# Eight tokens' gated one-hots made by one wide comparison and one wide product, in a Trainium2 decoder layer

## What is computed

```python
def peer_ffn(h, w_q, sub_keys1, sub_keys2, u_tab, v_tab):
    ...
    v1, i1 = lax.top_k(s1, PEER_TOPK)          # 16 of 128 keys, first half
    v2, i2 = lax.top_k(s2, PEER_TOPK)          # 16 of 128 keys, second half
    cand = (v1[..., :, None] + v2[..., None, :]).reshape(B, S, PEER_HEADS, PEER_TOPK * PEER_TOPK)
    cand_id = (i1[..., :, None] * N_KEYS + i2[..., None, :]).reshape(B, S, PEER_HEADS, PEER_TOPK * PEER_TOPK)
    top_s, pos = lax.top_k(cand, PEER_TOPK)
    ids = jnp.take_along_axis(cand_id, pos, axis=-1)
    g = jax.nn.softmax(top_s, axis=-1)
    ...
        u = jnp.take(u_tab, ix, axis=0)
        act = jax.nn.gelu(jnp.einsum('td,tkd->tk', hx, u), approximate=False)
        vv = jnp.take(v_tab, ix, axis=0)
        return jnp.einsum('tk,tkd->td', gx * act, vv)
```

## Time and profile before

| | |
|---|---|
| Median of 3 runs | 3248.29 us (3245.39 to 3252.73) |
| The profiled execution's own time | 3245.96 us |
| Its span | 3244.2 us |
| PE busy | 3109.5 us (96%) |
| DVE busy | 2455.2 us (76%) |
| ACT busy | 1056.3 us (33%) |
| POOL busy | 1026.5 us (32%) |
| Chain that ended last, by engine | PE 75%, DVE 18%, DMA 3% |

### The profile page before, as it was taken

One profiled execution on the slowest core, in us unless ns is written; L12 is line 12 of the kernel. 1 busy time (PEld: TensorE's weight loads), 2 busy tenths in 40 slices (PEclk: granted clock), 3 DMA queues, 4 the chain that ended last, 5 costly groups with the idle time before them and its releaser, 6 DMA issues.

```text
span 3244.2 us, 43813 instructions
## 1 busy us (share of the span) xinstructions
PE 3109.5 (96%) x16016; PEld 2659.8 (82%) x16016; DVE 2455.2 (76%) x3452; ACT 1056.3 (33%) x1632; POOL 1026.5 (32%) x734
## 2 busy tenths in 40 slices
PE   6999999999999999999999999999999999999994
PEld 4778887666469999997777899998999999999983
DVE  2397655645639999978888777888888888888757
ACT  1323545422223334332223333333333323333331
POOL 0110000000026553523222233435555554545200
PEclk9999999999999999999999999999999999999997
DMA  9786114465144555459888888888999899988853
GB/s 363 283 297 227 59 59 158 167 242 187 56 155 136 181 169 196 155 196 336 284 295 284 273 275 297 301 309 319 341 336 338 303 333 337 337 314 325 286 174 117
DMA packets 277725, 795.07 MB, mean 245 GB/s; under 512 B 118272, under 2 KB 138960, under 8 KB 230864
## 3 DMA queue, kind: packets, MB, share of 16 engines
q1 hardware_dynamic: 218816, 465.73, 42.6%
q0 software_dynamic: 50560, 317.87, 26.2%
q10 hardware_dynamic: 8208, 9.56, 0.8%
HBM read 750.07 MB, written 43.02 MB: 244 GB/s over the span
## 4 chain that ended last, share of the span: by engine, by line
PE 75%; DVE 18%; DMA 3%; issue 2%; ACT 1%; SPq 0%; POOL 0%; DVEq 0%; POOLq 0%; ACTq 0%
PE ps L2276 28%; PE ps L2212 26%; PE ps L1935 12%; DVE arena L1685 4%; PE ps L2187 3%; DVE arena L1682 2%; DMA arena<-in_w_ada 1%; DVE arena L1263 1%; PE ps L1959 1%; DVE arena L1710 1%; DVE split L1780 1%; PE ps L1894 1%; PE ps L1994 1%; PE ps L1871 1%; DVE win_parts L1250 1%
## 5 line engine op out<-in xcount | busy, mean ns | idle before, releaser
L2276 PE MATMUL ps<-split,w_parts 128*128 128x512 f32 x4608 | 1070.9, 392 | 20.0 <-DVE split L1780 17.2
L2276 PEld LDWEIGHTS ps<-split,w_parts 128*128 128x128 f32 x4608 | 863.8, 188 | 216.8 <-DVE split L1780 19.0
L2212 PE MATMUL ps<-h_parts,split 128*128 128x384 f32 x5376 | 947.4, 335 | 2.0 <-POOL split L788 1.4
L2212 PEld LDWEIGHTS ps<-h_parts,split 128*128 128x128 f32 x5376 | 933.7, 188 | 5.9 <-issue 1.6
L1125 ACT ACTIVATE split<-below_parts 128x1024 fp32r<-128x1024 f32 x416 | 441.7, 1062 | 1203.3 <-PE ps L2276 711.6
L1780 DVE TENSOR_TENSOR split<-below_parts,split 128x1024 fp32r<-128x1024 f32 x416 | 509.2, 1224 | 256.7 <-ACT split L1125 251.7
L800 POOL COPY arena<-arena 128x1 uint32 x256 | 209.8, 819 | 694.8 <-DVE arena L1734 389.4
L1715 DVE CUSTOM_DVE_ANT_0 arena<-arena 128x2048 f32<-128x2048 f32 x128 | 293.2, 2291 | 22.8 <-DMA arena<-in_u_tab,arena 22.8
L1734 DVE SCALAR_TENSOR_TENSOR arena<-arena 128x2048 f32<-128x2048 f32 x128 | 300.6, 2349 | 4.3 <-DVE arena L1726 2.2
L803 POOL DMA_INDIRECT arena<-in_v_tab,arena x128 | 257.4, 2011 | 104.4 <-POOL arena L800 103.1
L1250 DVE TENSOR_TENSOR win_parts<-arena,win_parts 128x512 fp32r<-128x512 f32 (+2 forms) x208 | 128.3, 629 | 210.5 <-ACT win_parts L854 201.3
(11 more groups left out here) (275 smaller groups left out, 3221.2 us busy)
## 6 DMA issues: line engine op xcount, KB each, us to landing
below_parts<-in_u_units SPq DMA_DIRECT2D x256, 512.0 KB, 4.7
below_parts<-in_v_tab SPq DMA_DIRECT2D x256, 512.0 KB, 6.9
arena<-in_w_ada SPq DMA_DIRECT2D x96, 1024.0 KB, 7.2
arena<-in_w_slices POOLq DMA_DIRECT2D x56, 512.0 KB, 4.6
gates_by_expert<-arena SPq DMA_DIRECT2D x24, 1024.0 KB, 4.8
below_parts<-gates_by_expert SPq DMA_DIRECT2D x32, 768.0 KB, 9.1
arena<-in_w_out POOLq DMA_DIRECT2D x32, 512.0 KB, 5.5
acts_ahead<-arena ACTq DMA_DIRECT2D x48, 192.0 KB, 2.1
```

Of the source, the lines that this page charges most:

```text
L2212: ins = nc.tensor.matmul(ps[:, 6 + b, 0:DT], lhs[:, cols], h2_parts[:, rhs, k, :], start=k == 0 and n == 0, stop=k == KT - 1 and n == 2)
L2276: ins = nc.tensor.matmul(ps[:, g.bank_of(half, m) + b, :], w_parts[:, buf, lhs, i, m * P:(m + 1) * P], rhs[:, b * 512:(b + 1) * 512], star ...
```

## The change

The comparison of the plain one-hots (L1682) stays. The eight `tensor_scalar` of a set, one per token, each of which compared `iota` with the token's second keys and multiplied by its gates in one go, are replaced by two `tensor_tensor` over all eight tokens: a comparison that writes ones and zeros, and a product in place with the gates. The product waits on a new semaphore `hot_made` for the comparison. So that the number of semaphores stays the same, `firsts_set` is gone, and the one place that used it counts on `c_made` (2 increments before, 3 now).

```diff
-            nc.vector.tensor_tensor(firsts[:, :], firsts[:, :], ident[:, 96:97], ALU.add).then_inc(firsts_set, 1)
+            nc.vector.tensor_tensor(firsts[:, :], firsts[:, :], ident[:, 96:97], ALU.add).then_inc(c_made, 1)
...
                     hot, first = one_hot[n % HOTS], m * P + n * OH
                     dve.wait_ge(g_ps, (first + OH) // 4)
                     nc.vector.tensor_tensor(hot[:, 0, :, :], over(iota[:, :], 1, OH), over(pick_cols[:, 0, first:first + OH], 2, NKEY), ALU.is_equal)
-                    for t in range(OH):
-                        at_t = first + t
-                        ins = nc.vector.tensor_scalar(hot[:, 1, t, :], iota[:, :], pick_cols[:, 1, at_t:at_t + 1], pick_cols[:, 2, at_t:at_t + 1],
-                                                      ALU.is_equal, ALU.mult)
-                    ins.then_inc(hot_ready, 1)
+                    nc.vector.tensor_tensor(hot[:, 1, :, :], over(iota[:, :], 1, OH), over(pick_cols[:, 1, first:first + OH], 2, NKEY), ALU.is_equal)\
+                        .then_inc(hot_made, 1)
+                    dve.wait_ge(hot_made, first // OH + 1)
+                    nc.vector.tensor_tensor(hot[:, 1, :, :], hot[:, 1, :, :], over(pick_cols[:, 2, first:first + OH], 2, NKEY), ALU.mult)\
+                        .then_inc(hot_ready, 1)
...
-            pe.wait_ge(firsts_set, 1)
+            pe.wait_ge(c_made, 3)
```

More of the change, by code:

```diff
@@ L567, in decoder_layer @@
             "cols_ps cols_ready hot_ready g_ps g_staged pre_high pre_split pre_used pre_gelu high_done unit_split unit_used "
-            "tile_gelu w_made w_high w_ready v_read picks_w tail_loaded gate_row_ps gate_row gate_stored ada_row firsts_set x1_ready y_ready "
+            "tile_gelu w_made w_high w_ready v_read picks_w tail_loaded gate_row_ps gate_row gate_stored ada_row hot_made x1_ready y_ready "
             "out_done var_ready root_ready"
@@ L577, in decoder_layer @@
          pre_high, pre_split, pre_used, pre_gelu, high_done, unit_split, unit_used, tile_gelu, w_made, w_high, w_ready, v_read,
-         picks_w, tail_loaded, gate_row_ps, gate_row, gate_stored, ada_row, firsts_set, x1_ready, y_ready, out_done, var_ready,
+         picks_w, tail_loaded, gate_row_ps, gate_row, gate_stored, ada_row, hot_made, x1_ready, y_ready, out_done, var_ready,
          root_ready) = map(sem, names.split())
```

## The result

| | before | changed |
|---|---|---|
| median of 7 runs each | 3248.57 us (3238.36 to 3254.20) | 3262.24 us (3257.53 to 3269.84) |
| ratio, 95% interval | | 1.0045 (1.0027 to 1.0063), +14.6 us (+8.8 to +20.5) |
| profiled execution, span | 3244.2 us | 3255.8 us |
| stage: first product of a set (L2233) to the first of the stream (L2276) | 355.77 us | 372.33 us |

The account below looks back on a forecast made before the run. VectorE was taken to bound the sets, 1099 to 1426 us. Terms 0.7 + 5.3 + 14.1 - 0.5 gave 19.6 us more, 3267.9 against the runs' median; forecast 3267 us, range 3257 to 3274.

Parts of the forecast that it names:

- VectorE is the bound from the first returned buffer to the last set: From 1099.19 to 1426.10 us the chain runs through VectorE alone, so a microsecond more there delays the end equally.
- The eight narrow operations cost 2.06 us a set, a wide one 1.135: In each VectorE set: eight tensor_scalar removed, 2.06 us; comparison and product added at a pitch of 1.135 us each.
- The wait costs 0.22 us: Between comparison and product in each set: 0.14 us for the semaphore plus the lost overlap of 0.08 us.
- POOL's turn stays at 2.1 us: In the sets, each POOL subtraction would still hold VectorE up by 2.1 us with wide operations.
- the sum: Total delay over the sets: 0.7 + 5.3 + 14.1 - 0.5 = 19.6 us.
- The rival in which wide operations are not held up: In VectorE's sets, POOL delays only narrow operations; PE's 8.3 us of waits go, about 3240 us; chance 0.06.
- The opening costs 0.7 us: Block 0's first four sets, made ahead: 3.5 us more, 2.2 absorbed by the buffer wait; counted 0.7 (0 to 1.3).
- A quarter of a turn comes back: In blocks 1 and 2 VectorE comes later against PE, so less of POOL's turn falls into the sets: -0.5 us.
- The renaming costs nothing: At PE's wait, c_made's third increment comes from the same VectorE instruction that gave firsts_set: no cost.
- PE waits 28 us for sets, in all blocks: Sign in the changed trace: PE's waits for sets rise from 8.3 to some 28 us, block 0's last pairs included.
- near 1446: Sign in the changed trace: the last set starts near 1446 us in place of 1426.

Follow-up runs that it names:

- sixteen_narrow: The kernel before with each of a set's eight narrow operations split in two over 64 keys; stage 426.45 us against 355.77.
- held_between: The changed kernel with one more semaphore instruction between the wait for hot_made and the product; stage 376.63 us against 372.33.

## Why the prediction was right, point by point

- *VectorE is the bound from the first returned buffer to the last set, and a microsecond there is one at the end.* Right for the stage's end. Its part of the chain, 1091.25 us to the start of the last set on PE at 1434.72, is 343.5 us against 326.9 before, and the stage grew by the same 16.6. sixteen_narrow shows it for 70.7 us.
- *The eight narrow operations cost 2.06 us a set, a wide one 1.135.* Right, to 0.01 us; the product in place costs 1.14.
- *The wait costs 0.22 us (0.14 and the overlap).* The term that was mis-sized: 0.12 us. The 0.14 was read from rows of `Steps`, which puts a semaphore instruction behind the wait; the change has a bare wait, 0.03 us. held_between put that instruction in: 0.14 us, and 4.3 us more in the stage. A set costs 0.34 us more, not 0.44: 15.0 us in place of 19.4 over 44 sets.
- *POOL's turn stays at 2.1 us.* 2.19 for 2.08 in the sets shown. Over all 44 sets from the fifth on, VectorE took 192.9 us before and 207.6 now; less 44 undisturbed sets, that leaves 52.5 us for 25 turns before and 52.3 for 24 now, 2.10 and 2.18 us each. That is +1.9 us that the sum lacked; why a turn costs more is open. The rival in which wide operations are not held up fell with the first row of 3.40 us.
- *The opening costs 0.7 us.* The four sets made ahead swallowed it: VectorE was idle 0.4 us before the fifth where it had been idle 2.2, so nothing of it went through in the changed kernel.
- *A quarter of a turn comes back.* A whole one did in the sets: in VectorE's sets of block 1, 10 subtractions of POOL started before and 9 now, -2.1 us. But another fell on `gates_of(1)`, which the sum did not look at. Between block 0's last set and block 1's first, VectorE took 64.6 us before and 66.4 now, 1.8 us more, and line 1670, 0.29 us before, shows why:

```profile
1149.81 1.97 DVE L1670 TENSOR_TENSOR arena<-arena 128x128 f32<-128x128 f32 x1 [0.50 <-DVE arena L1669]
1149.26 2.38 POOL L788 TENSOR_TENSOR w_parts<-below_parts,w_parts 128x1024 fp32r<-128x1024 f32 x1 [6.36 <-ACT w_parts L1088]
```

- With these, 15.0 + 1.9 - 2.1 = 14.8 us in the sets, which is what they grew by (4.4, 4.3 and 6.1 in the three blocks), and 1.8 between them: 16.6, as measured. The 19.6 of the sum came nearer to that than its terms did: 4.4 for the wait, 0.7 for the opening and 1.6 more of a turn back are 6.7 us less, and 1.9 for the turns and 1.8 for `gates_of(1)` stand against it.
- *The renaming costs nothing, and all behind the last set goes on as before.* Right: 26.88 us from the last set to the stream in both. The rest of the kernel scatters by 22 us over the profiles (1791 to 1813), more than the change is worth. The last set started at 1434.72 us and not near 1446: the stage itself began 7.9 us early, and the sum was 3 us too high.
- *PE waits 28 us for sets, in all blocks.* 24.4, the last two pairs of block 0 among them, and the clock stayed at 1.00 with waits of up to 1.5 us. It fell where the waits were longer: in sixteen_narrow (up to 4.8 us) to 0.90 on average over 1240 to 1310 us, where PE was busy 54.36 of 70 us.

## What to carry to other kernels

Counting instructions is not counting time. A fused narrow operation that compares and multiplies at the double rate can beat two wide ones, and the fixed 0.19 us per instruction has to be set against the rate and against the second pass. Take the price of a wait from rows with the same instructions around it. And where two engines exchange turns, look at which of them does the work: 1.14 us of subtraction on VectorE were cheaper than letting POOL take a turn of 2.1 us. Compare engines over the whole period in which they come round to the same point, not over the burst in which one is seen waiting.

## What the runs showed of the hardware that I had not expected

- Two wide VectorE operations with a bare semaphore wait between them stand 0.03 us apart, 0.12 us of pitch over none; with one semaphore instruction in between, 0.14 us.
- POOL's memset of 128 x 1024 (0.95 us) held up none of the 54 two-input operations that ran beside one, but narrow operations of 0.335 us stood at up to 1.207.
- The stage repeated to 0.02 us (355.77 and 355.75) between two executions of unchanged work that took 3245.96 and 3253.65 us in whole, so a profile can settle differences that rounds of timing can't. Where waits for stores came in, the repeat was off by 1.3 us.
